# Four lists of rows instead of two for the accumulating writes of the experts, freed by a semaphore that GpSimd counts up

## The reference

```
top_i, top_w = route(h2, p["w_router"], p["router_bias"])       # 8 of 64 experts per token
# assignments sorted by expert, each expert's rows padded to blocks of 128 rows
def block(args):
    tok, e = args                                               # 128 token numbers, one expert
    return swiglu(h_pad[tok], w_gate[e], w_up[e], w_down[e])    # (128,1024) -> (128,256) -> (128,1024)
out = lax.map(block, (row_tok.reshape(n_blocks, MOE_BLOCK), blk_exp))
out = out.reshape(n_rows, D) * row_w[:, None]                   # weight of the assignment
ffn = jax.ops.segment_sum(out, row_tok, num_segments=T + 1)[:T] + swiglu(h2, w_sh_gate, w_sh_up, w_sh_down)
```

## Time and profile before

| | |
|---|---|
| median of three runs | 2126.03 us |
| profiled execution | 2128.7 us, span 2127.1 us |
| TensorE busy in the span | 91% (matmul), 71% (weight load) |
| VectorE, ScalarE, GpSimd busy | 49%, 41%, 19% |
| stage of the experts | about 1103 to 2063 us |
| `final` behind it | 64 us |

### The profile page before, as it was taken

How to read it: one execution, slowest core, us unless ns; L and a number is a source line. 1 busy time by engine, 2 the same in 40 slices (tenths; PEclk the granted TensorE clock), 3 DMA queues, 4 the chain that set the end, 5 groups by cost and what they waited for, 6 DMA issues and landing times. The chain is left out here.

```text
span 2127.1 us, 33716 instructions
## 1 busy us (share of the span) xinstructions
PE 1928.6 (91%) x10176; PEld 1507.9 (71%) x10177; DVE 1044.8 (49%) x1519; ACT 872.1 (41%) x1181; POOL 414.0 (19%) x337
## 2 busy tenths in 40 slices
PE   3799999899899999989789999999899999999960
PEld 3799999899888666755446777666566777777740
DVE  3212411155337334545336666565566666666646
ACT  4210111234203222211246666666566666666642
POOL 0100000111111000001112333333233333223320
PEclk9899999999899999999899999999999999999985
DMA  6211221011263666325069999999999999979946
GB/s 240 71 50 40 82 96 30 30 60 43 68 209 117 216 219 212 138 86 195 19 257 380 306 292 294 356 318 379 374 327 345 286 286 286 275 233 310 279 91 259
DMA packets 154836, 433.67 MB, mean 204 GB/s; under 512 B 11551, under 2 KB 76307, under 8 KB 130210
## 3 DMA queue, kind: packets, MB, share of 16 engines
q1 hardware_dynamic: 120338, 307.40, 38.6%
q0 software_dynamic: 31776, 116.05, 21.1%
q10 hardware_dynamic: 2672, 9.57, 1.2%
HBM read 351.27 MB, written 81.72 MB: 204 GB/s over the span
## 5 line engine op out<-in xcount | busy, mean ns | idle before, releaser
L2038 DVE TENSOR_TENSOR wexp_lo<-wexp,wexp_hi 128x2048 fp32r<-128x2048 f32 x190 | 426.9, 2289 | 49.3 <-ACT wexp_hi L1990 44.4
L1990 ACT ACTIVATE wexp_hi<-wexp 128x2048 fp32r x190 | 353.2, 1907 | 54.4 <-issue 52.9
L1971 PE MATMUL bank<-wexp_down,hTe 128*128 x736 | 331.0, 592 | 1.8 <-ACT ob L2016 1.8
L1946 PE MATMUL bank<-wexp_hi,x_hi 128*128 128x512 f32 x744 | 300.0, 403 | 3.8 <-DVE wexp_lo L2038 3.8
L1946 PE MATMUL bank<-wexp_hi,x_lo 128*128 128x512 f32 x744 | 291.5, 392 | 0.0
L1946 PE MATMUL bank<-wexp_lo,x_hi 128*128 128x512 f32 x744 | 290.0, 390 | 0.0
L1920 POOL DMA_INDIRECT acc_d<-ob,ixs x92 | 153.0, 1663 | 599.8 <-DMA acc_d<-ob,ixs 290.9
L1971 PEld LDWEIGHTS bank<-wexp_down,hTe 128*128 128x128 f32 x736 | 138.8, 189 | 142.4 <-issue 135.5
L494 PE MATMUL bank<-hT_hi,w_hi 128*128 128x344 f32 x576 | 187.7, 326 | 3.3 <-DVE w_lo L578 3.3
L494 PE MATMUL bank<-hT_hi,w_lo 128*128 128x344 f32 x576 | 185.7, 322 | 0.0
L494 PE MATMUL bank<-hT_lo,w_hi 128*128 128x344 f32 x576 | 185.1, 321 | 0.0
(11 more groups left out here) (338 smaller groups left out, 2917.3 us busy)
## 6 DMA issues: line engine op xcount, KB each, us to landing
wexp<-in_w_exp_gate SPq DMA_DIRECT2D x64, 1024.0 KB
wexp<-in_w_exp_up SPq DMA_DIRECT2D x64, 1024.0 KB
wexp_down<-in_w_exp_down SPq DMA_DIRECT2D x64, 1024.0 KB
wada<-in_w_ada SPq DMA_DIRECT2D x12, 2048.0 KB, 10.9
w_raw<-in_w_in SPq DMA_DIRECT2D x44, 512.0 KB, 3.9
gates_d<-gst POOLq DMA_DIRECT2D x48, 172.0 KB, 2.1
gate<-gates_d SPq DMA_DIRECT2D x16, 516.0 KB, 5.5
xn<-in_x_prompt ACTq DMA_DIRECT2D x8, 512.0 KB
```

Source lines behind the costliest of these rows:

```text
L1946: last = pe.matmul(banks[0][:].rearrange("p (g n) -> p g n", g=2), stat[:, b, k, :], mov[:, b, :, k * FF:(k + 1) * FF], start=(k == 0 and ...
L1971: last = pe.matmul(banks[4 + half][:], hT[:, f, :], wdn[:, bass.ds(slot, 1), f, half * 512:half * 512 + 512].rearrange("p a n -> p (a n)") ...
L1990: act.activation(w_hi[:, b, g, :], wexp[:, bass.ds(e & (RING - 1), 1), g, :].rearrange("p a n -> p (a n)"), ACT.Copy).then_inc(whi_ok, 1)
L2038: dve.tensor_tensor(w_lo[:, b, g, :], wexp[:, bass.ds(e & (RING - 1), 1), g, :].rearrange("p a n -> p (a n)"), w_hi[:, b, g, :], ALU.subtr ...
```

## The change

Four lists `ixs` stand in place of two, indexed by the block's place in the ring of four. A new semaphore, `landed`, starts at 3 and is raised by GpSimd in each block once its wait for the add before has been passed, right before it issues its own add; the instruction takes the place of one that raised `passed`. VectorE waits for `landed` at i + 1, which asks for the landing of the add of block i - 4, in place of `added` for block i - 2. ScalarE waits for `landed` at i + 3 in place of `ixs_ok`, which asks for the landing of the add of block i - 2 as before. VectorE's wait for the zeroing ahead of its loop is gone.

```
-        ixs = [tile(f"ixs{b}", [P, 1], U32) for b in range(2)]
+        ixs = [tile(f"ixs{q}", [P, 1], U32) for q in range(RING)]
+        landed = sem("s6landed")
...
                 tidy(pool)
+                pool.sem_inc(landed, RING - 1)
...
                     pool.wait_ge(added, 16 * i + 32)
-                    pool.sem_inc(passed, 1)
-                    pool.indirect_dma_start(out=acc_d, out_offset=bass.IndirectOffsetOnAxis(ap=ixs[b][:, 0:1], axis=0),
+                    pool.sem_inc(landed, 1)
+                    pool.indirect_dma_start(out=acc_d, out_offset=bass.IndirectOffsetOnAxis(ap=ixs[q][:, 0:1], axis=0),
...
                     act.wait_ge(wc_ok, i + 1)
-                    act.wait_ge(ixs_ok, i + 1)
+                    act.wait_ge(landed, i + 3)
...
-                def to_add(j, b):
-                    dve.tensor_copy(ixs[b][:], lists[:, bass.ds(j, 1)]).then_inc(ixs_ok, 1)
+                def to_add(j, q):
+                    dve.tensor_copy(ixs[q][:], lists[:, bass.ds(j, 1)]).then_inc(ixs_ok, 1)
...
-                    dve.wait_ge(added, 16 * i + 16)
+                    dve.wait_ge(landed, i + 1)
                     dve.sem_inc(passed, 1)
-                    to_add(i, b)
+                    to_add(i, q)
...
-                dve.wait_ge(added, 32)
                 blocks(dve, block_of)
```

## The result

The changed kernel takes 2132.36 us in the median of nine runs (2129.79 to 2136.9), the kernel before 2126.03 (2123.18 to 2129.59): ratio 1.0031, 95% interval 1.0019 to 1.0042. So it is about 6.6 us slower by the ratio, 6.3 by the medians; the forecast was 2132.4. The profiled execution took 2132.36 us, with a span of 2130.7. In the new file the add stands in L1922, the gather in L1905, `hh` in L2046, `ixs` in L2052, `wexp_lo` in L2040, `ob` in L2018 and TensorE's down product in L1973.

A forecast was written before the change was run, and what follows sets the result against it. In the stretch a chain of GpSimd's adds, each issued some 0.8 us behind the landing before, bounds the kernel. Terms -2.1 + 5.5 + 2.5 - 2.0 + 2.5 = +6.4 on the median 2126.0 give 2132.4 us, range 2122.5 to 2141.

The forecast's parts named there:

- the stretch: 1317.88 to 1653.53 in the experts' stage, where adds set the pace and 25.0 us are lost against 10.02 per block.
- The places of the link: Predicted times of instructions after an add's landing in the stretch: `hh` at L+3.5, transposes L+5.7, `wexp_lo` from L+6.1.
- The nearer TensorE, -2.1: In the stretch TensorE's transposes start at L+5.7, not L+7.80; 2.1 us won once at the exit near 1646.
- L: The landing of an add, from which the other instructions of its link are timed, in us.
- Before the stretch, +5.5: Adds from 1200.55 to 1309.25 meet running subtractions, six hit and a last touch under 0.1; 5.5 us slower.
- The hits: GpSimd's issues of adds that meet a running `wexp_lo` subtraction and wait for its end, longer than the usual 1.58 us.
- the walk: Stepping down the adds before the stretch, each moved by losses so far, against `wexp_lo` windows: +5.5, or about +3.8.
- Inside the stretch, +2.5 and -2.0: Issues after five short links lose 0.5 us each, +2.5; the old hit at 1507.50 goes, -2.0.
- the rival, given 0.12: Weights load too early into full DMA engines, stretching each of 26 long links by 0.2: 5.2 us more, 2137.6; chance 0.12.
- Behind the stretch, +2.5: 25 adds from 1653.45 to 1901.33 delayed by hits, less TensorE's distance; +2.5 us taken from 0 to 9.
- every delay of an issue is passed on whole: Each add is issued on the landing of the one before, so any delay moves all that follow by its full size.
- The lock: GpSimd's issue of an add waits for a VectorE operation with two SBUF inputs, held for the whole instruction; 1.96 us at 1507.50.

The follow-up runs named there:

- Experiment 1: Changed kernel with VectorE's wait made as strict as before (landed at i + 3); 2126.69 us against 2126.99 for the kernel before, ratio 0.9998.
- Experiments 3 and 4: Changed kernel, each subtraction of 2048 columns cut into four of 512 (3: 2128.82 us, ratio 1.0011) or two of 1024 (4: 2124.9 us, ratio 0.9991).
- Experiment 2: Changed kernel with SyncE's gate and up loads held until the first half of the next block's wexp_hi is rounded; 2124.66 us, ratio 0.9993.
- experiment 9: Changed kernel with a second VectorE wait (landed at i + 3) right ahead of the subtractions wexp_lo; 2153.68 us, ratio 1.0127.
- experiment 11: Kernel before with two register reads on GpSimd ahead of each add and two on VectorE behind `ixs`; 2173.42 us, ratio 1.0222.
- Experiment 6: Changed kernel with the subtractions cut into sixteen pieces of 256 columns; 2143.37 us, ratio 1.009.

## Why the prediction was right, and where its steps were not

**Right.** The sign, the size and the cause at its root: VectorE freed of the wait runs its subtraction into GpSimd's issues, 25 of them (20 to 35 were given), 24 us (over 10). Experiment 1 shows that the loss comes from this freedom. ScalarE's wait did move to GpSimd, but it is 113.9 us in the stretch, not about 75. The places of the link held within 0.4 us, except `wexp_lo` (1.1 sooner) and the gate load (0.6 sooner).

**The nearer TensorE, -2.1:** the transposes stand at L+5.7 as given, because two small errors cancel: `ob` comes 0.3 sooner, and the down product starts 0.43 to 0.46 behind `hTe`. At the exit the stage won 3.0 against the chain (8.5 less 5.5). The other 0.9 is not distance: add 47 landed in 6.05 us where it took 10.07 before, so the chain let go one link sooner.

**Before the stretch, +5.5:** the ledger has +4.0 up to add 21, out of two terms. The hits were 7.7; 1.7 of them, on adds 19 and 20 (1321.61 and 1333.48), lie in what the prediction calls the stretch. Up to add 19 hits are 6.0, landings 4.0 sooner, and the chain is only 1.9 longer. The hits are near the walk, though the start at 1198.00 fell on the very start of a subtraction and just missed it (for that case the walk gave +3.8 in all): from 1218.13 on the phases met heavily. Experiments 3 and 4 show them to be worth what they measure. Against them stand 3.6 to 4.5 us of sooner landings that VectorE's freedom brings with and without hits, a term that the prediction did not have. What makes these landings sooner was not isolated.

**Inside the stretch, +2.5 and -2.0:** the chain is 4.5 longer on adds 21 to 46, and 6.5 longer (301.9 against 295.4) from add 19 on, where the prediction's stretch begins. Only two of the short links' followers are hit, hard (3.67 and 3.48 long) instead of five a little: 4.0 where before had 2.0, so +2.0, not +0.5. Adds 19 and 20, behind long links that were said to be clear by 1.1, bring 1.7 more. Another +2.5 is landings, nearly all of it one add that lands in 8.38 us and not in some 6.4, beside loads that are issued 7 us earlier against L. Experiment 2 gives back 4.5 us of landings by moving the loads, and 3.3 of hits with them, so alone it does not tell the two apart. In experiments 3 and 4 the hits are 2.7 and 2.9, hardly over the 2.0 of before, and the chain is still 5.6 and 4.2 longer than before. So early loads have a part, as the rival, given 0.12, supposed, but not in its way: it stretched each of 26 long links by 0.2, and the long landings kept their length. That the loads are the larger part in the stretch is the likely reading of one profile each; it is not shown. The rule of the Trainium skill (DMA: Bandwidth & Descriptors, on arbitration), by which a deeper backlog of weights would cost the adds nothing, is not contradicted by these rows: a long landing took 10.49 us in the mean before and 10.51 after.

**Behind the stretch, +2.5:** 0. The hits are there (11.5 us on adds 46 to 91, before 4.5), but TensorE's distance and the sooner landings take them all.

**The step that failed** is the sum inside the stretch, in what it was made of: it put +2.5 of hits there and left the early loads, "bytes per block don't change", at nothing. Moving only the loads took 7.7 us off the chain there (experiment 2). In the terms of the prediction the places were -2.1, +5.5, +0.5 and +2.5, in sum +6.4; the runs have -3.0, +1.9, +6.5 and 0, in sum +5.4. That the total is within 1 us is luck: the place inside the stretch is 6.0 over, the others 0.9, 3.6 and 2.5 under. With this step goes the sentence that every delay of an issue is passed on whole: it holds for the few us of hits ahead of the stretch, but in the stretch only 8% (experiment 9) to 21% (experiment 11) arrives, and of large delays ahead of it 41 to 64%. Ahead of the stretch it also left out the sooner landings, -3.6.

**The lock.** The Trainium skill (SBUF — State Buffer, on the two separate sides) has the lock for a VectorE operation with two SBUF inputs only against a GpSimd operation that reads SBUF, a condition that the prediction left out. The traces agree in that the held issues end behind the instruction that they meet: 1.58 us became 3.67 at most in the changed kernel, beside instructions of 2.29, and 5.60 beside one of 4.43. The other way round these rows show no hold: the subtraction begun at 1451.92, inside the issue of 1451.10 to 1452.68, took its usual 4.49. Experiment 6 goes beyond the page: a train of short instructions could hold GpSimd as long as one long one.

**A trap in reading.** In the stretch after, six of TensorE's down products name the load of `wexp_down` as what ended their wait:

```profile
1625.80 3.70 PE L1973 MATMUL bank<-wexp_down,hTe 128*128 x8 [1.29 <-DMA wexp_down<-in_w_exp_down]
```

That looks like a late load. But each starts 0.43 to 0.46 behind the end of `hTe` (here 1625.33), like those that name `hTe` (1469.07 behind 1468.64). The wait is for `hTe`, which comes behind `ob`; the load landed in the meantime.

## What to carry to other kernels

A wait that costs nothing on the critical path can keep two engines out of each other's way: before it is removed, find what the freed engine will run beside, and what it will release sooner (here a lock on GpSimd's issues, and loads 7 us earlier into full DMA engines). When it is removed, both can be mended, here by subtractions of 1024 columns and by a load that waits for a later event: either alone took the loss back, and with both the kernel is 0.34% faster than before. How much of that the freedom itself brings is open, since four pieces and late loads were not tried on the kernel before. And a delay in a chain of transfers is to be priced by a measured rate, not passed on whole, since a transfer issued late beside a burst of loads lands sooner after its issue.

## What the runs showed of the hardware that was not expected

- An indirect transfer's issue on GpSimd (1.58 us alone) can wait for a whole train of VectorE's short instructions with two SBUF inputs (begun 0.34 us apart): 4.75 us at most, in 12 of 27 long issues of that profile. With instructions of 1024 columns (1.22 us) no issue was longer than 2.65.
- Beside full DMA engines the landing hardly follows the issue: of 28.2 us of added lateness over 25 links 22.4 came back as shorter landings.
- GpSimd's gathers gained from the change: 1638 ns in the mean before, 1275 after, as fewer of them meet a subtraction (32 long ones after, 55 before). It bought nothing, since they are not on the chain.
